# Reordering the edges of a woven mLSTM stage: the gate work at its start and the output gating at its end

## The reference

```python
qk, v, o, gates = split(h @ w_in)            # h: latent and context tokens
qk = silu(depthwise_conv(qk, conv_w, conv_b))  # 5 taps
q, k = split(qk); q, k = axial_rope(q), axial_rope(k)   # latent tokens only
# ig, lf from gates; chunks of 128; 8 heads; forward and backward
h_f = mlstm_chunkwise(q, k, v, ig_f, lf_f, state_f)
h_b = reversed mlstm_chunkwise of the reversed inputs
h = rms_norm(h_f + h_b) * sigmoid(o)
x = x + g1 * (h @ w_out)
```

## Time and profile before

| | |
|---|---|
| time, three runs | 1733.72, 1736.02 (median), 1740.56 us |
| profiled execution | 1740.56 us, its span 1738.7 us |
| TensorE busy | 1662.0 us, 96% of the span |
| VectorE, ScalarE, GpSimd busy | 1021.9, 668.8, 77.4 us |
| chain that ended last | TensorE 86%, VectorE 5%, DMA 3%, ScalarE 3% |
| mean granted TensorE clock | 0.984 of full |

### The profile page before, as it was taken

The page is one execution under the profiler, slowest core; times in us unless marked ns, Lnnn a source line. Parts: engine busy times, 40 slices in busy tenths (PEclk is TensorE's granted clock), DMA queues, the critical chain, the costliest instruction groups (busy, mean ns, idle before and its releaser), DMA issues.

```text
span 1738.7 us, 26390 instructions
## 1 busy us (share of the span) xinstructions
PE 1662.0 (96%) x10284; PEld 1407.1 (81%) x10284; DVE 1021.9 (59%) x1586; ACT 668.8 (38%) x1185; POOL 77.4 (4%) x118
## 2 busy tenths in 40 slices
PE   5999999889799999999999989999999899999997
PEld 4888878668699899899999767777777688888885
DVE  4787777543896388368448555766554534343434
ACT  4434444442443144234224343544574422222222
POOL 0331011000200000000000000000000000000000
PEclk8999999999999999999999999999999999999999
DMA  8622333122124422522431531110113223232333
GB/s 341 71 89 98 134 122 110 38 87 66 39 76 146 146 74 94 186 85 73 165 112 64 198 121 49 37 49 25 49 61 133 73 97 121 97 121 97 109 109 133
DMA packets 49557, 177.86 MB, mean 102 GB/s; under 512 B 5552, under 2 KB 5808, under 8 KB 49328
## 3 DMA queue, kind: packets, MB, share of 16 engines
q1 hardware_dynamic: 33712, 123.86, 21.1%
q10 hardware_dynamic: 14976, 51.52, 8.2%
q0 software_dynamic: 768, 1.08, 0.9%
HBM read 172.21 MB, written 4.19 MB: 101 GB/s over the span
## 4 chain that ended last, share of the span: by engine, by line
PE 86%; DVE 5%; DMA 3%; ACT 3%; issue 1%; SPq 0%; POOL 0%; ACTq 0%; DVEq 0%
PE PS L590 34%; PE PS L2119 16%; PE PS L2242 9%; PE PS L2430 8%; PE PS L2094 3%; PE PS L2285 2%; DMA scr<-in_ada 2%; PE PS L2085 2%; PE PS L2518 1%; PE PS L2301 1%; PE PS L2517 1%; PE PS L2101 1%; PE PS L2385 1%; PE PS L2181 1%; PE PS L2267 1%
## 5 line engine op out<-in xcount | busy, mean ns | idle before, releaser
L561 DVE TENSOR_TENSOR w_lo<-raw,w_hi 128x1024 fp32r<-128x1024 f32 x172 | 211.1, 1228 | 125.3 <-ACT w_hi L556 119.1
L556 ACT ACTIVATE w_hi<-raw 128x1024 fp32r<-128x1024 f32 x172 | 181.2, 1054 | 231.5 <-PE PS L590 180.9
L590 PE MATMUL PS<-c_hi,w_hi 128*128 128x512 f32 (+1 forms) x672 | 207.4, 363 | 6.5 <-DVE w_lo L561 5.5
L590 PE MATMUL PS<-c_hi,w_lo 128*128 128x512 f32 (+1 forms) x672 | 204.3, 358 | 0.0
L1348 DVE SCALAR_TENSOR_TENSOR X<-PS,mod,X 128x512 f32<-128x512 f32 (+1 forms) x120 | 75.7, 659 | 218.6 <-PE PS L590 208.9
L590 PE MATMUL PS<-c_lo,w_hi 128*128 128x512 f32 (+1 forms) x672 | 203.9, 357 | 0.0
L590 PE MATMUL PS<-h_hi,w_hi 128*128 128x512 f32 x368 | 139.2, 385 | 3.9 <-DVE w_lo L561 3.9
L590 PE MATMUL PS<-h_lo,w_hi 128*128 128x512 f32 x368 | 139.0, 385 | 0.0
L590 PE MATMUL PS<-h_hi,w_lo 128*128 128x512 f32 x368 | 138.9, 384 | 0.0
L590 PEld LDWEIGHTS PS<-c_hi,w_hi 128*128 128x128 f32 x672 | 111.6, 190 | 31.4 <-DVE w_lo L561 8.6
L1653 DVE SCALAR_TENSOR_TENSOR c_early<-X,small,c_early 128x798 f32<-128x798 f32 x120 | 125.9, 1050 | 2.9
(11 more groups left out here) (346 smaller groups left out, 3096.9 us busy)
## 6 DMA issues: line engine op xcount, KB each, us to landing
raw<-in_w SPq DMA_DIRECT2D x192, 512.0 KB, 3.4
adaw<-in_ada ACTq DMA_DIRECT2D x64, 512.0 KB, 4.2
adaw<-in_w SPq DMA_DIRECT2D x20, 512.0 KB, 4.1
scr<-in_ada ACTq DMA_DIRECT2D x16, 512.0 KB, 6.4
scr<-in_ada SPq DMA_DIRECT2D x4, 1024.0 KB, 14.8
c_early<-in_ada SPq DMA_DIRECT2D x4, 1024.0 KB, 19.3
X<-in_xT SPq DMA_DIRECT2D x4, 768.0 KB, 6.7
X<-in_xT ACTq DMA_DIRECT2D x1, 3072.0 KB, 10.1
```

What stands on the lines that cost most here:

```text
L556: nc.scalar.activation(w_hi[:, j], raw[:, j].rearrange("p (k n) -> p k n", k=KT), ACT.Copy).then_inc(s_hi, 1)
L561: nc.vector.tensor_tensor(w_lo[:, j], raw[:, j].rearrange("p (k n) -> p k n", k=KT), w_hi[:, j].bitcast(f32), ALU.subtract).then_inc(s_lo, 1)
L590: last = nc.tensor.matmul(G[j][:, a:b], w[:, j, k], m[:, k, a:b], start=(n == 1), stop=(n == 3 * k_tiles))
```

## The change

At the start of the stage silus(0) on ScalarE moves ahead of ml_out(2), and v_augmented(0, 0) ahead of ml_out(3). On VectorE ml_split(4) moves behind rope(0) and keys_weighted(0) ahead of ml_split(5). On TensorE rotate(0) and transpose_values(0, 0) move into product 3, and transpose_keys(0) ahead of product 4.

At the end ml_split(20) moves behind exponentials2(14) on ScalarE and behind weighted(14) on VectorE. The slots of unit 15 are cut elsewhere and the last four transpose_head calls move later. After the units, head_norm(7) comes before o_sigmoid(5) and o_hi(3), the order of the output gating and of the splits of rows 24 and 25 changes on ScalarE and VectorE, and the reload of X is issued after o_hi(7). gate_pair waits for both splits and both evictions at its head and takes k-tiles 0 to 5 of both outputs in turn.

```diff
--- before.py
+++ after.py
@@ -137,7 +137,7 @@
         i = WOVEN + n
         return ((i, 0, 4),), ((i, 4, 8),)
     return {12: (((18, 0, 6),), ((18, 6, 8), (19, 0, 4))), 13: (((19, 4, 8), (20, 0, 2)), ((20, 2, 8),)),
-            14: (((21, 0, 6),), ((21, 6, 8), (22, 0, 4))), 15: (((22, 4, 8), (23, 0, 4)), ((23, 4, 8),))}[n]
+            14: (((21, 0, 6),), ((21, 6, 8), (22, 0, 4))), 15: (((22, 4, 8), (23, 0, 2)), ((23, 2, 8),))}[n]
 
 
 def biased_count(U):
@@ -1215,15 +1215,15 @@
             ml_out(0)
             ml_split(3)
             ml_out(1)
+            silus(0)
             ml_out(2)
             ml_split(4)
-            silus(0)
             act.wait_ge(s_g2, 18)
             nc.scalar.activation(ge[:].rearrange("p a n -> p (a n)"), ge[:].rearrange("p a n -> p (a n)"), ACT.Exp)\
                 .then_inc(s_g3, 1)
+            v_augmented(0, 0)
             ml_out(3)
             ml_split(5)
-            v_augmented(0, 0)
             v_augmented(0, 1)
             ml_out(4)
             ml_split(6)
@@ -1235,7 +1235,6 @@
                     ml_out(5 + n)
                 elif n == 13:
                     ml_out(18)
-                    ml_split(20)
                 elif n == 14:
                     ml_out(19)
                     ml_out(20)
@@ -1246,6 +1245,8 @@
                     exponentials2(n + 1)
                 if n <= 12:
                     ml_split(7 + n)
+                if n == 13:
+                    ml_split(20)
                 if hp < 3:
                     if u == 0:
                         silus(hp + 1)
@@ -1265,22 +1266,22 @@
                         o_sigmoid(o)
                     o_hi(2)
                     ml_split(23)
+                    nc.scalar.preload_act_table_set(LOG_EXP)
+            head_norm(7)
             o_sigmoid(5)
             o_hi(3)
-            nc.scalar.preload_act_table_set(LOG_EXP)
-            head_norm(7)
+            ml_out(22)
+            o_sigmoid(6)
             ml_split(24)
             o_hi(4)
             o_hi(5)
+            ml_out(23)
+            o_sigmoid(7)
+            ml_split(25)
+            o_hi(6)
+            o_hi(7)
             act.wait_ge(s_hT, 8)
             act.dma_start(X[:, :, 0:LAT], x_spill).then_inc(s_back, 16)
-            ml_out(22)
-            o_sigmoid(6)
-            ml_split(25)
-            ml_out(23)
-            o_sigmoid(7)
-            o_hi(6)
-            o_hi(7)
             out_proj(1)
             ffn()
             for j in range(2):
@@ -1983,17 +1984,17 @@
             step(V.scalar_tensor_tensor(out=ge[:, 2], in0=bb[:, 0], scalar=-1.0, in1=rcol, op0=ALU.mult, op1=ALU.subtract))
             step(V.tensor_scalar(nga, ga, -1.0, None, ALU.mult))
             short_conv(0, 1)
-            ml_split(4)
             dve.wait_ge(s_g1, 6)
             step(V.tensor_copy(nrow.rearrange("p d n -> p (d n)"), PS[0:48, 4, 256:512]))
             assert g2[0] == GD_END, g2[0]
             dve.wait_ge(s_spill, 16)
             dve.wait_ge(s_trig, 16)
             rope(0)
+            ml_split(4)
             dve.wait_ge(s_g3, 4)
             decays(0)
+            keys_weighted(0)
             ml_split(5)
-            keys_weighted(0)
             states(0, 0)
             short_conv(1, 0)
             masked(0)
@@ -2001,8 +2002,6 @@
             ml_split(6)
             for n in range(16):
                 hp, u = n // 4, n % 4
-                if n == 13:
-                    ml_split(20)
                 if n < 15:
                     masked(n + 1)
                 if u == 0:
@@ -2036,16 +2037,16 @@
                     o_gated(2)
                     o_lo(2)
                     ml_split(23)
-                    o_gated(3)
+            o_gated(3)
+            o_gated(4)
             o_lo(3)
-            o_gated(4)
+            ml_split(24)
             o_gated(5)
-            ml_split(24)
             o_lo(4)
             o_lo(5)
             o_gated(6)
+            o_gated(7)
             ml_split(25)
-            o_gated(7)
             o_lo(6)
             o_lo(7)
             dve.wait_ge(s_back, 16)
@@ -2185,11 +2186,11 @@
 
             def gate_pair():
 
-                steps = [(k, 0) for k in range(6)] + [(k, 1) for k in range(3)] + [(6, 0), (7, 0)] + [(k, 1) for k in range(3, 8)]
+                pe.wait_ge(s_lo, R_O1 + 2)
+                pe.wait_ge(s_gf[0], R_O1 // 2)
+                pe.wait_ge(s_gf[1], R_O1 // 2)
+                steps = [(k, j) for k in range(6) for j in range(2)] + [(k, j) for j in range(2) for k in (6, 7)]
                 for k, j in steps:
-                    if k == 0:
-                        pe.wait_ge(s_lo, R_O1 + j + 1)
-                        pe.wait_ge(s_gf[j], R_O1 // 2)
                     pe.wait_ge(s_ocat, k + 1)
                     for n, (x, m) in enumerate(((w_hi, c_hi), (w_hi, c_lo), (w_lo, c_hi))):
                         last = MM(G[j][:, 0:LAT], x[:, j, k], m[:, k, 0:LAT], start=(k == 0 and n == 0),
@@ -2551,11 +2552,13 @@
             for d in range(2):
                 last = MM(PS[0:48, 4, 256 + 128 * d:384 + 128 * d], rcol[:, 48 * d:48 * d + 48], ident, start=True, stop=True)
             last.then_inc(s_g1, 1)
-            ml_product(3)
+            ml_product(3, 0, 2)
             rotate(0)
+            ml_product(3, 2, 4)
             transpose_values(0, 0)
+            ml_product(3, 4, 8)
+            transpose_keys(0)
             ml_product(4)
-            transpose_keys(0)
             transpose_values(0, 1)
             ml_product(5, 0, 4)
             updates(0, 0)
@@ -2570,9 +2573,6 @@
                     if u % 2:
                         key_query((n + 1) // 2)
                 outputs(n)
-                if n == 15:
-                    transpose_head(4)
-                    transpose_head(5)
                 first, second = unit_slots(n)
                 for part in first:
                     ml_product(*part)
@@ -2583,7 +2583,7 @@
                         transpose_keys(hp + 1)
                     elif u == 3:
                         updates(hp + 1, 0)
-                for o in {13: (0,), 14: (2,), 15: (6, 7)}.get(n, ()):
+                for o in {13: (0,), 14: (2,), 15: (4, 5)}.get(n, ()):
                     transpose_head(o)
                 for part in second:
                     ml_product(*part)
@@ -2594,7 +2594,7 @@
                         transpose_values(hp + 1, 1)
                     elif u == 3:
                         updates(hp + 1, 1)
-                for o in {13: (1,), 14: (3,)}.get(n, ()):
+                for o in {13: (1,), 14: (3,), 15: (6, 7)}.get(n, ()):
                     transpose_head(o)
 
             out_proj(1)
```

## The result

The changed kernel takes 1759.2 us (median of 4 runs, 1756.2 to 1762.2) against 1736.2 us for the kernel before (the three runs already shown and a fourth): ratio 1.0127, 95% interval 1.0102 to 1.0151, which is +22 us (+18 to +26). It is slower, as forecast; the forecast was 1756.3 us, or +20.3. The profiled execution took 1756.63 us with a span of 1754.8. That is only 16.1 us more than the one of before, which was the slowest of its kernel.

The account below looks back on a forecast made before the run. TensorE was taken to bound the kernel, with next to no slack. Front 10.1, product 20 2.0 and tail 8.2 summed to 20.3 us on a median of 1736.0: 1756.3 us, range 1747 to 1763.

Parts of the forecast that it names:

- TensorE as the bound: Whole stretch: TensorE has next to no slack, 5.0 us of waits in all, so late releases come back as time.
- the first rival: Between front and tail: TensorE catches up and absorbs late starts there; 1736 to 1744 us, chance 3%.
- The rival that the tail hides itself: Tail: reload or head wait overlaps idle time, only half of 8.2 us is left; 1752 us, chance 10%.
- The front: Stage's start: product 3 7.7 us late, 0.5 before product 4, 1.9 of clock loss; 10.1 us together.
- The second rival: Before product 3: no wait, because the conv steps end 7.7 us earlier on VectorE; 1746.2 us, chance 4%.
- The table load: ScalarE after silus(0): 1.28 us for the load by the profile row, without the skill page's 1.38 us of drain.
- Product 20: Loop's end: product 20 starts 2.0 us late, waiting for its w_lo; clock loss taken as 0.
- the rival that the clock falls more often: After product 20's wait too, and longer after the others: up to 5.5 us more, 1762 us, chance 15%.
- gate_pair's head: Tail: TensorE waits 6.1 us at gate_pair's start for the w_lo of row 25, then 1.9 us of clock loss.
- The reload: Tail: X, issued later, is back at 1326.1 after 10.6 us; gate_pair's first output comes last, at 1327.0.
- The tail's sum: Stage's end: product 2 of the output projection starts 8.2 us late, bounds 6.3 to 9.9 us.
- The sum: Whole kernel: front 10.1, product 20 2.0 and tail 8.2 make 20.3 us more.

Follow-up runs that it names:

- tail_only: All edits of the stage's end except ml_split(20), made on the kernel before: ratio 1.0060, +10.4 us.
- silus_only: The kernel before with one line moved, silus(0) ahead of ml_out(2) on ScalarE: ratio 1.0057, +9.9 us.
- after_early_reload: The changed kernel with the reload of X issued earlier, between o_hi(4) and o_hi(5): ratio 1.0140 to the kernel before.
- split20_only: The kernel before with only ml_split(20) moved, behind exponentials2(14) and weighted(14): ratio 1.0017, +3.0 us.
- front_only: The kernel before with all edits of the stage's start and none of its end: ratio 1.0060, +10.4 us.
- both weaves: The kernel before with the edits of the stage's start except the move of silus(0), timed twice: ratios 1.0010 and 1.0028, +1.7 and +4.9 us.
- swap_only: The kernel before with only ml_out(4) moved ahead of v_augmented(0, 1) on ScalarE: ratio 0.9981, -3.3 us.
- gate_only: The kernel before with only gate_pair changed, its waits at the head and its list of steps: ratio 1.0039, +6.8 us.
- tail_old_gate: The kernel before with the edits of tail_only, but gate_pair left as before: ratio 1.0057, +9.9 us.

## Why the prediction was right, and where its sizes were off

- **TensorE as the bound** held. All three parts were paid in full, and no idle time between 1085 and 1270 was there to give them back (the first rival): the waits there are 1.1 us in all before and 0.9 now, besides the 1.48 before product 5. The parts' sum of 23.8 us lies within the whole's interval, 18 to 26. The rival that the tail hides itself, with only half of 8.2 us left, is out by tail_only's interval, 6.8 to 14.0.
- **The front** was forecast with 7.7 + 0.5 + 1.9 = 10.1 us. It was 7.7, 0.34 before product 4 and 2.3 of clock in the trace, and 10.4 us (7.5 to 13.5) by time. silus_only showed that the moved line is the cause. The second rival needed the conv steps to end 7.7 us earlier; counted from the stage's first matmul they ended 0.7 us earlier.
- **The table load.** The load starts at 1063.17, 0.02 us after the second Silu's end, and ml_out(2) starts at 1064.46, 0.01 us after the load's end at 1064.45, so the row decided. By the figure of the Trainium skill (ScalarE: Activation LUTs, What ACT_TABLE_LOAD costs) another 1.38 us of drain would belong to the switch; this trace doesn't agree.
- **Product 20** was forecast with 2.0 us and no clock loss. The wait was 1.94, but the clock did fall (1.7 us). I had put that loss at nothing because the wait was short. It fell in all three traces that have this wait (the changed kernel, after_early_reload, split20_only). That the 1.7 us of the old dip at 1166 went away in the same execution, so that the sum hid it, was luck. It is a part of the rival that the clock falls more often.
- **gate_pair's head**: 6.1 us forecast, 5.83 measured. In its clock loss I had 1.9 and it was 2.5.
- **The reload** is hidden in the changed kernel, as forecast: back at 1334.0, wanted at 1336.4. after_early_reload showed it by moving it. It went out 1.3 us before gate_pair started and not together with it: the trace has its issue at 1322.88, while the two copies written ahead of it (L1205) run from 1322.80 to 1323.93.
- **The tail's sum** was forecast with 8.2 us. The trace gives 21.0 - 10.5 = 10.5 us from product 20 to product 2, of which 1.7 is product 20's clock loss, so 8.8 against that one execution of before; the time of tail_only gives 10.4 (6.8 to 14.0). The term that was mis-sized is its starting point. I measured from a product 2 that waited 2.03 us behind a reload of 11.9 us. In the six experiments whose tail is the old one (front_only, silus_only, both weaves, split20_only, swap_only) the reload took 10.0 to 10.9 us, and the wait was 0.37 to 1.03 us. Behind these waits the clock stayed at 1.00, where it had fallen behind the 2.03 us. By these six the kernel before was better than the one execution that I read, by 1.0 to 1.7 us at product 2's start and by 1.7 us of clock behind it. Against the best of them, with a wait of 0.37 us, the traces give gate_only 2.74 + 1.7 + (2.41 - 0.37) = 6.5 us (6.8 by time) and tail_only 5.82 + 6 x 0.43 of clock + 2.04 = 10.4 us (10.4 by time); against a wait of 1.03 they are 0.7 us less.
- **The sum** of 20.3 us was 1.7 under the measured 22: the tail's term was too low by some 2 us and product 20's by 1 to 1.7, and the whole came out less than its parts. So the total is better than its terms, and that is in part luck.
- **Against the profiled execution** I had 1760.9 and it was 1756.6; against the median 1756.3 and it was 1759.2. Both forecasts lie within the spread of the changed kernel's executions, 1756.2 to 1762.2, and the single execution can't tell them apart.

What was only argued: that the timed runs of the kernel before had the short waits and the full clock of the six traces. Timed runs have no trace, and the kernel before itself has one only. Why the reload takes 9.8 us at one time and 11.9 at another was not tested.

## What to carry to other kernels

Where one engine is busy nearly all the time (TensorE here 96% of the span), price a reordering by one question at each of its waits: which instruction releases it, and what now stands ahead of that one in its own queue. A copy that frees the accumulator must not stand behind an instruction that waits for another engine's chain; here that one line cost 9.9 us. Two late things that meet at one point cost the later of them, so repairing either alone brought next to nothing here (after_early_reload, tail_old_gate). And a term that rests on one transfer's latency in one execution needs its spread before it is trusted to a microsecond.

## What the runs showed of the hardware that was not expected

- The same 2048 KB reload took from 9.8 to 11.9 us in the thirteen traces that have it in one piece, 11.9 in the one first read. Cut in two, its first quarter landed after 4.4 us.
- The length of the wait alone didn't decide whether the clock fell. In the kernel before there are two waits of 0.55 us: behind the one at 1165.67 the clock fell (0.57 over 4 us), behind the one at 1222.49 it stayed at 1.00. Behind 1.94 us it fell (0.57 over 4 us in split20_only), behind 2.03 in the kernel before and behind 2.74 in gate_only as well (0.57 over 4 us each), but behind 2.41 us it stayed at 1.00 (the changed kernel, gate_only, tail_only), and behind 1.48, too (from 1081 in the earlier trace rows). Behind 5.8 and 8.1 us it fell in each of the four traces of the changed kernel, front_only, silus_only and tail_only, to a mean of 0.53 to 0.61 over 6 us. TensorE stood idle for the named time before each of these. What decides between the short ones these traces don't settle.
